# Seven block products in place of eight in the last output projection of a three-layer transformer kernel

## The reference, cut to what matters

```python
y_sb = stick_breaking_attention(qh, kh, vh) ... * jax.nn.silu(g_sb)
y_lru = rg_lru(xc, ...) * jax.nn.silu(g_lru)
y = jnp.concatenate([y_sb, y_lru], axis=-1)          # (512, 2048)
h = h + jnp.einsum('bse,ed->bsd', y, w_out[l])       # w_out 2048 x 2048
```

## Time and profile before

| what | value |
|---|---|
| median of three timed runs | 2098.05 us (2097.89 to 2100.16) |
| profiled execution, first to last instruction | 2098.9 us |
| mean granted TensorE clock of that execution | 0.999 |
| TensorE busy | 2082.9 us, 99% |
| VectorE, ScalarE, GpSimd busy | 1417.7, 996.4, 191.2 us |
| DRAM traffic | 210.33 MB read, 24.12 MB written |

### The profile page before, as it was taken

How to read it: one execution, slowest core, us unless ns; L and a number is a source line. 1 busy time by engine, 2 the same in 40 slices (tenths; PEclk the granted TensorE clock), 3 DMA queues, 4 the chain that set the end, 5 groups by cost and what they waited for, 6 DMA issues and landing times. The chain is left out here.

```text
span 2098.9 us, 30066 instructions
## 1 busy us (share of the span) xinstructions
PE 2082.9 (99%) x9702; PEld 1734.5 (83%) x9702; DVE 1417.7 (68%) x2581; ACT 996.4 (47%) x1928; POOL 191.2 (9%) x197
## 2 busy tenths in 40 slices
PE   9999999999999999999999999999999999999999
PEld 7888888888888888888888788888888888888887
DVE  6677777777733568888888633677777677868432
ACT  6444444445422446666666633544454545446221
POOL 0111111112101000000000122200000000003000
PEclk9999999999999999999999999999999999999999
DMA  7324444445733624444444734533434334345742
GB/s 227 100 72 113 111 112 114 113 114 170 210 83 97 196 63 122 126 127 127 127 127 118 250 95 115 170 106 86 121 101 133 87 108 119 109 114 156 218 112 70
DMA packets 409917, 264.40 MB, mean 126 GB/s; under 512 B 20480, under 2 KB 382720, under 8 KB 409856
## 3 DMA queue, kind: packets, MB, share of 16 engines
q1 hardware_dynamic: 401120, 255.87, 43.1%
q10 hardware_dynamic: 8736, 7.74, 1.5%
HBM read 210.33 MB, written 24.12 MB: 112 GB/s over the span
## 5 line engine op out<-in xcount | busy, mean ns | idle before, releaser
L639 PE MATMUL pp<-act_hi,w_hi 128*128 128x512 f32 x2304 | 903.1, 392 | 6.9 <-DVE w_lo L613 4.2
L641 PE MATMUL pp<-act_hi,w_lo 128*128 128x512 f32 x2304 | 898.2, 390 | 0.0
L640 PE MATMUL pp<-act_lo,w_hi 128*128 128x512 f32 x2304 | 897.9, 390 | 0.0
L613 DVE TENSOR_TENSOR w_lo<-raw,w_hi 128x512 fp32r<-128x512 f32 x680 | 457.1, 704 | 360.7 <-ACT w_hi L605 359.8
L605 ACT ACTIVATE w_hi<-raw 128x512 fp32r<-128x512 f32 (+1 forms) x684 | 396.2, 622 | 456.2 <-PE pp L641 231.3
L639 PEld LDWEIGHTS pp<-act_hi,w_hi 128*128 128x128 f32 x2304 | 433.1, 188 | 100.9 <-DVE w_lo L613 6.0
L641 PEld LDWEIGHTS pp<-act_hi,w_lo 128*128 128x128 f32 x2304 | 432.9, 188 | 91.1
L640 PEld LDWEIGHTS pp<-act_lo,w_hi 128*128 128x128 f32 x2304 | 433.2, 188 | 87.3 <-issue 0.2
L658 POOL TENSOR_TENSOR pT_lo<-gathered,pT_hi 128x640 fp32r<-128x640 f32 x30 | 46.5, 1571 | 358.9 <-ACT pT_hi L654 358.9
L1318 ACT ACTIVATE prob<-ps,minus,q_scale 128x512 f32<-128x512 f32 (+1 forms) x64 | 39.0, 615 | 78.3 <-DVE minus L1398 78.3
L639 PE MATMUL ps<-act_hi,w_hi 128*128 128x512 f32 x176 | 69.3, 394 | 0.0
(11 more groups left out here) (435 smaller groups left out, 2755.1 us busy)
## 6 DMA issues: line engine op xcount, KB each, us to landing
raw<-w_in SPq DMA_DIRECT2D x48, 1024.0 KB, 5.9
raw<-swa_w_in SPq DMA_DIRECT2D x36, 1024.0 KB, 5.8
raw<-mla_w_in SPq DMA_DIRECT2D x23, 1024.0 KB, 5.7
raw<-mla_w_out SPq DMA_DIRECT2D x16, 1024.0 KB, 6.5
raw<-swa_w_out SPq DMA_DIRECT2D x16, 1024.0 KB, 6.1
raw<-w_out SPq DMA_DIRECT2D x16, 1024.0 KB, 6.9
gathered<-turned SPq DMA_DIRECT2D x224, 56.0 KB, 2.0
x_feature_major<-xT SPq DMA_DIRECT2D x8, 1024.0 KB, 9.7
```

Source lines behind the costliest of these rows:

```text
L613: q.eng.tensor_tensor(dst, raw_piece(tile, p), high, ALU.subtract).then_inc(s_lo, tile.ups(p))
L639: q.eng.matmul(psum[:, :], wh, ah, start=start and n == 0, stop=False)
L640: q.eng.matmul(psum[:, :], wh, al, start=False, stop=False)
L641: last = q.eng.matmul(psum[:, :], wl, ah, start=False, stop=stop and n == PIECE // P - 1)
```

## The change

Units 2 to 7 of `out3` are computed by seven block products. The 256 outputs of a unit form two rows of blocks (its two tiles), the 2048 inputs two halves (8 chunks each), the 512 tokens two halves (256 each, `early` and `late`). A plain unit has eight products of a weight block (128 outputs x 1024 inputs) with a block of y (1024 inputs x 256 tokens). Strassen's scheme (in Winograd's form) makes seven products, from the weight blocks 11, 12, 22, from four sums of weight blocks s1 to s4, and from the blocks of y and four sums of them. The steps:

- GpSimd makes the four sums of y once (`y_sums_G`: `chain`, then `chain`, `after`, `before`; 2048 elements per partition each), first from the recurrence half that it already holds, then with chunks 8 to 15, which are read again from DRAM into `xT`. ScalarE and VectorE split each of them (`y_sums_A`, `y_sums_V`).
- GpSimd makes the four sums of weight blocks of every unit (1024 elements per partition), two of them in place in `raw`, and adds the partial products that several outputs share to the scaled old x (four sums of 256 elements a unit).
- ScalarE and VectorE split seven blocks of 1024 elements a unit (before: eight pieces of 512 elements), into a ring of four slots.
- TensorE multiplies with 256 columns (`strassen_T`), each block product in a bank of its own, in the order 11, 12, s1, s2, s3, s4, 22.
- VectorE adds up the products from PSUM in seven sums of 256 columns a unit (`strassen_V`).
- SyncE loads four blocks of 512 KB a unit as their places in `raw` come free, and the old x, second half, after the sums of y are split.

```diff
-          "out3": (KC // 2, KC // 2, 2)}
+          "out3": (2, KC // 2, 2)}
+PLAIN_LAST = 2
+HALF_K, HALF_S = KC // 2, S // 2
+PRODUCTS = ("11", "12", "s1", "s2", "s3", "s4", "22")
+RING = (2, 3, 0, 1)
...
+        def strassen_dmas(q, old_x):
...
+            q.eng.dma_start(xT[:, HALF_K:KC - 1, :], y_dram[HALF_K:KC - 1].rearrange("c p s -> p c s")).then_inc(s_ycopy, 16)
+            q.eng.wait_ge(s_lo, Tile("out3", PLAIN_LAST - 1, 1).count(PIECES - 1))
+            for b in ("11", "12", "22", "21"):
+                block(PLAIN_LAST, b)
...
+            for i in range(PLAIN_LAST, units):
+                n = i - PLAIN_LAST
+                if i + 1 < units:
+                    q.eng.wait_ge(s_wsum, 4 * n + 3)
+                    q.eng.wait_ge(s_wlo, split_of(i, "11"))
+                    block(i + 1, "11")
+                    q.eng.wait_ge(s_wlo, split_of(i, "s3"))
+                    block(i + 1, "21")
+                    q.eng.wait_ge(s_wlo, split_of(i, "s4"))
+                    block(i + 1, "12")
+                    q.eng.wait_ge(s_wlo, split_of(i, "22"))
+                    block(i + 1, "22")
+                store_out(q, i, 0)
+                store_out(q, i, 1)
...
+        def strassen_T(q):
+            for i in range(PLAIN_LAST, KC // 2):
...
+                for product in PRODUCTS:
+                    q.eng.wait_ge(s_wlo, split_of(i, product))
...
+                    for c in range(HALF_K):
+                        cols = slice(c * P, (c + 1) * P)
+                        m = products(q, product_bank(product), (high[:, cols], low_[:, cols]), y_of(product, c),
+                                     c == 0, c == HALF_K - 1)
+                    m.then_inc(s_product, 1)
...
+        def y_sums_A(q):
...
+                q.eng.wait_ge(s_tsum, (1, 3, 3, 4)[n])
...
+                q.eng.activation(dst, src, ACT.Copy).then_inc(s_thi, 1)
...
+        def y_sums_V(q):
...
+                q.eng.wait_ge(s_thi, n + 1)
+                q.eng.tensor_tensor(dst, src, high.bitcast(F32), ALU.subtract).then_inc(s_tlo, 1)
...
+        def y_sums_G(q):
...
+            q.eng.wait_ge(s_yload[0], 16 * LAYERS)
+            q.eng.tensor_tensor(chain[:, 0:last, :], y_lru[:, :, late], y_lru[:, :, early], ALU.subtract)
+            q.eng.tensor_tensor(chain[:, last, :], d_y[:, 1, late], d_y[:, 1, early], ALU.subtract).then_inc(s_tsum, 1)
+            q.eng.wait_ge(s_ylo_v, y_lo_count(KC - 1))
+            again = xT[:, KC - 1, :]
+            q.eng.tensor_tensor(again, act_hi[:, KC - 1, :].bitcast(F32), act_lo[:, KC - 1, :].bitcast(F32), ALU.add).then_inc(s_ycopy, 1)
+            q.eng.wait_ge(s_ycopy, 17)
+            q.eng.wait_ge(s_tlo, 1)
+            q.eng.tensor_tensor(chain, after, chain, ALU.subtract).then_inc(s_tsum, 1)
+            q.eng.wait_ge(s_tsum, 2)
+            q.eng.tensor_tensor(after[:, 0:last, :], after[:, 0:last, :], y_lru[:, :, late], ALU.subtract)
+            q.eng.tensor_tensor(after[:, last, :], after[:, last, :], d_y[:, 1, late], ALU.subtract).then_inc(s_tsum, 1)
+            q.eng.tensor_tensor(before, before, chain, ALU.subtract).then_inc(s_tsum, 1)
...
+        def strassen_A(q):
+            for product in PRODUCTS[0:4]:
+                split_hi(q, PLAIN_LAST, product)
+            for i in range(PLAIN_LAST, KC // 2):
...
+                q.eng.activation(p1_sum, product_bank("11"), ACT.Copy).then_inc(s_part, 1)
+                for product in PRODUCTS[4:]:
+                    split_hi(q, i, product)
+                if i + 1 < KC // 2:
+                    for product in PRODUCTS[0:4]:
+                        split_hi(q, i + 1, product)
...
+        def strassen_V(q):
...
+            for i in range(PLAIN_LAST, KC // 2):
+                n, more = i - PLAIN_LAST, i + 1 < KC // 2
+                split_lo(q, i, "s3")
+                new(i, "12", 0, early, 1)
+                split_lo(q, i, "s4")
+                split_lo(q, i, "22")
...
+                q.eng.tensor_tensor(q_sum, product_bank("s2"), p1_sum, ALU.add).then_inc(s_sums, 1)
+                q.eng.wait_ge(s_sums, 3 * n + 1)
+                q.eng.tensor_tensor(u_sum, product_bank("s1"), q_sum, ALU.add).then_inc(s_sums, 1)
+                if more:
+                    scale_old(i + 1)
+                    split_lo(q, i + 1, "11")
+                new(i, "s3", 1, late, 2)
+                q.eng.tensor_tensor(q_sum, product_bank("s3"), q_sum, ALU.add).then_inc(s_sums, 1)
+                if more:
+                    split_lo(q, i + 1, "12")
+                new(i, "s4", 0, late, 3)
+                if more:
+                    split_lo(q, i + 1, "s1")
+                new(i, "22", 1, early, 4)
+                if more:
+                    split_lo(q, i + 1, "s2")
...
+        def strassen_G(q):
...
+                    if s == "s1":
...
+                        m = q.eng.tensor_tensor(w_sum, raw_block("21"), raw_block("22"), ALU.add)
...
+                    if s == "s2":
+                        q.eng.wait_ge(s_wlo, split_of(i, "s1"))
+                        m = q.eng.tensor_tensor(w_sum, w_sum, raw_block("11"), ALU.subtract)
...
+            sums(PLAIN_LAST, "s1", "s3", "s2")
+            for i in range(PLAIN_LAST, KC // 2):
+                n = i - PLAIN_LAST
+                sums(i, "s4")
+                q.eng.wait_ge(s_part, n + 1)
+                q.eng.wait_ge(s_old, n + 1)
+                add(i, 0, early, p1_sum)
+                q.eng.wait_ge(s_sums, 3 * n + 2)
+                add(i, 1, late, u_sum)
+                add(i, 0, late, u_sum)
+                q.eng.wait_ge(s_sums, 3 * n + 3)
+                add(i, 1, early, q_sum)
+                if i + 1 < KC // 2:
+                    sums(i + 1, "s1", "s3", "s2")
...
+            if n == LAYERS:
+                y_sums_A(q)
+                strassen_A(q)
+                return
...
             q.eng.wait_ge(s_xload[0], 16 * n)
+            if n == LAYERS:
+                y_sums_V(q)
+                m = [q.eng.scalar_tensor_tensor(xT[:, j, :], xT[:, j, :], g("gf", j), rstd_f[:, :], ALU.mult, ALU.mult)
+                     for j in (2 * PLAIN_LAST, 2 * PLAIN_LAST + 1)][-1]
+                m.then_inc(s_old, 1)
+                for product in PRODUCTS[0:2]:
+                    split_lo(q, PLAIN_LAST, product)
+                unit(1)
+                for product in PRODUCTS[2:4]:
+                    split_lo(q, PLAIN_LAST, product)
+                strassen_V(q)
+                return
...
             y_lo(q, 3, range(10, 12))
+            y_sums_G(q)
+            strassen_G(q)
```

More of the change, by code:

```diff
@@ L403, in build @@
         acc_b = out_tok[:, 0, :, :].rearrange("p b n -> p (b n)")
+        with ExitStack() as scope:
+            sb("over_x", [P, KC, S], F32, scope)
+            t1, t2, t3 = (sb(n, [P, 2, HALF_K, HALF_S], F32R, scope) for n in ("t1", "t2", "t3"))
+        chain = low[:, 0:HALF_K * HALF_S].rearrange("p (c n) -> p c n", c=HALF_K)
+        w_sum = low[:, 8 * HALF_S:12 * HALF_S]
+        p1_sum, q_sum, u_sum = (low[:, (12 + n) * HALF_S:(13 + n) * HALF_S] for n in range(3))
         with ExitStack() as scope:
@@ L1549, in y_lo, with y_lo_count @@
                                     ALU.subtract).then_inc(s_ylo_g if j in Y_GPSIMD[n] else s_ylo_v, 1)
+        def y_lo_count(j):
+            by_vector = [m for m in range(KC) if m not in Y_GPSIMD[LAYERS]]
+            return KC * (LAYERS - 1) - sum(len(Y_GPSIMD[m]) for m in range(1, LAYERS)) + by_vector.index(j) + 1
         def y_split(q, n, j):
@@ new lines, in y_sums_G @@
+        def y_sums_G(q):
+            early, late = slice(0, HALF_S), slice(HALF_S, S)
+            before, after = y_sum_places()
+            last = HALF_K - 1
+            q.eng.wait_ge(*q.at("V.turned_lo", phase="stick", body=H3 - 1))
+            q.eng.wait_ge(*q.at("V.y_lru", phase="stick", body=H3 - 1))
+            q.eng.wait_ge(s_yload[0], 16 * LAYERS)
[11 more added lines that the diff above has]
+            q.eng.tensor_tensor(before, before, chain, ALU.subtract).then_inc(s_tsum, 1)
@@ new lines, in strassen_V, with scale_old, new @@
+        def strassen_V(q):
+            def scale_old(i):
+                if i == HALF_K // 2:
+                    q.eng.wait_ge(s_xload[1], 16 * LAYERS)
+                for k in range(2):
+                    old = xT[:, 2 * i + k, :]
+                    m = q.eng.scalar_tensor_tensor(old, old, g("gf", 2 * i + k), rstd_f[:, :], ALU.mult, ALU.mult)
+                m.then_inc(s_old, 1)
+            def new(i, product, k, cols, sums):
+                n = i - PLAIN_LAST
+                q.eng.wait_ge(s_product, split_of(i, product))
+                q.eng.wait_ge(s_oldsum, 4 * n + sums)
+                q.eng.wait_ge((s_out, s_out2)[k], 16 * i)
+                q.eng.tensor_tensor(x_new(i, k)[:, cols], product_bank(product), xT[:, 2 * i + k, cols], ALU.add).then_inc(s_new, 1)
+            early, late = slice(0, HALF_S), slice(HALF_S, S)
+            for i in range(PLAIN_LAST, KC // 2):
```

(17 more changed lines are left out.)

141 lines of the change are left out of this document (129 added, 12 removed).

## The result

The changed kernel takes 2134.2 us (median of 4 runs, 2132.9 to 2135.4); the kernel before takes 2099.1 in the same set. The ratio is 1.0163 [1.0149, 1.0178], slower by 1.6%. The profiled span is 2132.9 us, 34.0 above that of before.

The account below looks back on a forecast made before the run. TensorE's own pace was taken to bound the kernel; 3.4 + 19.7 + 2.3 + 13.9 - 9.8 - 0.3 = +29.2 us on the span of 2098.9 gave 2128.1, hence a forecast of 2127 us, range 2107 to 2140.

Parts of the forecast that it names:

- tail of the attention: Attention's end: GpSimd's first difference of y holds up VectorE's masking, delaying TensorE's transposes, +3.4 us (bounds 0 and 4.8).
- first block product: Start of unit 2: TensorE waits for y sums and splits ordered ahead of block 11's split, 19.7 us.
- unit 2, ahead of s2: Sum s2 must wait until VectorE has split s1, so TensorE gets s2's split late, +2.3 us.
- pace of units 3 to 7: GpSimd and VectorE turns plus stretches with neither make 22.9 us a unit; TensorE waits 2.8 us each, +13.9 us.
- lower clock in the last unit: No clock loss was added; a slower product was held to mostly eat waiting.
- columns saved: TensorE in six units: seven block products of 256-column products take 20.13 us for 21.76, -9.8 us in all.
- end: At the end VectorE's last sum takes 0.42 us for 0.69, -0.3 us.
- third cost: Units 3 to 7 slowed by GpSimd and VectorE taking turns in SBUF: 22.9 us a unit, +13.9 us.
- Rival (a): Only the start costs, units keep 20.13 us: +6.6 us, 2105 us; chance 0.15.
- Rival (b): Faster: y sums ready when unit 1 ends and pace held, whole 9.8 us remain, 2088 us; chance 0.04.
- (c): Units at a pace of 25.4 us, clock falling at each wait: +12 on the forecast, 2139 us; chance 0.10.
- (d): 256-column products held up by their weight loads, 0.19 us each, +59 us in all; chance 0.01.

Follow-up runs that it names:

- late difference: Changed kernel, but GpSimd's first difference of y waits until VectorE is through with the last attention body's masking; 2129.1 us, ratio 1.0143.
- copies on GpSimd: Changed kernel with each weight sum on GpSimd replaced by one-source copies, s1 to s4 split from copied blocks; 2122.0 us, one run.
- last kernel: All sums on VectorE, block 22 split earlier; against that, unit 3's sums and splits earlier, unit 1's second output put off to unit 4; 2098.0 us, ratio 0.9988.

## Why the prediction came out right

Its terms, against what the traces show:

| term | forecast | measured |
|---|---|---|
| tail of the attention | +3.4 | +3.9 (y's last step at 1945.13 for 1941.81, in a trace that runs 0.6 early) |
| first block product | +19.7 | +19.6 |
| unit 2, ahead of s2 | +2.3 | +2.2 (a wait of 0.5, 1.7 by the lower clock) |
| pace of units 3 to 7 | +13.9 (22.9 us a unit) | +17.0 (23.55, TensorE's own 20.16) |
| lower clock in the last unit | 0 | +1.5 |
| columns saved | -9.8 | -9.6 |
| end | -0.3 | not measured by itself |

With the -0.3 the measured terms make 34.3, less the 0.6 by which the trace runs early 33.7; the spans differ by 34.0. Of the 7 us between the forecast 2127 and 2134.2, 4.8 are these terms. The rest is the step from spans to times: in the set of the result the kernel before took 2099.1 us and not 2098.05, and the medians differ by 35.1 us where the spans differ by 34.0.

The mechanism of each cost was the one named. The tail was taken away by itself by the late difference, the pace by moving the weight sums. The first wait was taken away in parts: 4.1 us by moving the weight sums, 4.7 by moving the y sums, and the whole of it only with both and a new order of splits and loads, which left 5 to 6 us of later waits.

The step that was off is the size of the third cost, "I take 22.9 us per unit": 20.0 us of turns and 2.9 us in which neither engine has its turn. By the count above the turns fill 21.1 us of a unit and the stretches 2.5. VectorE's turn was taken as 0.98 us from a pair of 512 elements; beside a sum of 1024 it is 1.08, a split that meets no sum keeps its 1.21, and a GpSimd sum that meets a split loses 0.88. That more than makes up for the shorter stretches. They are 2.1 us from s2 to s2 at the full clock, 2.5 where the clock was lower for a part and 3.3 where the two loads came late, although the forecast had the loads hidden.

(The Trainium skill, SBUF — State Buffer, section Who interferes with whom, calls the ports that the two engines share an exclusive lock; that the lock lasts for the whole instruction it says of VectorE's 2-port performance modes. The runs bear out a lock for the whole instruction but for some 0.14 us: 1.08 for 1.22, and 0.88 for the 1.02 us that the split at 2008.54 still ran. The 25.3 us that the forecast drew from it was too much, since the PSUM sums, put in a row there, partly run beside GpSimd's.)

The other term that was off is the clock, put at nothing. Behind the waits of units 3, 5 and 7 some 16 products start 0.21 us apart, 1.5 us each time. The forecast held that a slower product mostly eats waiting. It does: TensorE then comes later to the next unit, which waits less (1.67 for 2.65 us) and keeps its clock. In unit 7 nothing follows, and the 1.5 us stay.

Rival (a), that only the start costs, is refuted for this kernel by its waits, though it is what is seen once the weight sums are on VectorE. Rival (b) would have wanted the y sums ready at unit 1's end; even with all sums on VectorE only 2.5 us of it were had. In (c) the clock fell, at three of five waits, but the pace was 23.55, not 25.4. (d) is refuted: the products start 0.12 us apart with a weight load for each.

## What to carry to other kernels

An engine's idle time in the profile is no room for more work if it shares its way into memory with another: add up what VectorE and GpSimd do in SBUF in one unit, add the time in which the order lets neither of them work (2.4 us of a unit here), and compare the sum with the bound. Work with two SBUF operands that GpSimd does at half of VectorE's speed shuts VectorE out for longer (2.40 us a sum) than VectorE itself would need for it (1.22). A saving on the bounding engine that needs preparation is paid at the first unit, where nothing covers it; count what has to be ready there, and by when.

## What was not expected of the hardware

A GpSimd copy with one source shuts VectorE's two-operand work out as a sum does (2.05 us for 1.22). The clock of TensorE fell behind waits of 3.61, 2.65, 2.95 and 2.68 us and not behind those of 1.67 in units 4 and 6; with copies on GpSimd it fell behind one of 2.0, and in the profiled run of the last kernel it did not behind one of 2.1. In the kernel with the late first difference it stayed high behind a wait of 2.71 us, ahead of unit 3's s2, and fell behind one of 2.67, ahead of unit 4's. Timelines of that kernel:

```profile
2018.00 0.39 PE L680 MATMUL pt<-t,w_hi 128*128 128x256 f32 x1 [2.71 <-DVE w_lo L1760]
2018.22 0.28 PE L681 MATMUL pt<-t,w_hi 128*128 128x256 f32 x1
...
2041.09 0.58 PE L680 MATMUL pt<-t,w_hi 128*128 128x256 f32 x1 [2.67 <-DVE w_lo L1760]
2041.47 0.42 PE L681 MATMUL pt<-t,w_hi 128*128 128x256 f32 x1
```

So the length of the wait alone does not decide it, and these runs do not show what does. At the lower clock a product of 256 columns with its weight load starts every 0.21 us, at the higher every 0.12: 1.8 and not 2 times.
